# Up projection in seven block products: the fourth product of the gate block summed in PSUM, one pair late, with two PSUM pairs in turn

## What is computed

```python
def conv_ffn(hn, buf, w_up, conv_w, conv_b, w_down):
    T = hn.shape[1]
    up = hn @ w_up
    full = jnp.concatenate([buf.astype(up.dtype), up], axis=1)
    conv = sum(full[:, j:j + T] * conv_w[j] for j in range(CONV_W)) + conv_b
    a, gt = jnp.split(conv, 2, axis=-1)
    return (a * jax.nn.silu(gt)) @ w_down, full[:, T:]
```

## Time and profile before

| | us |
|---|---|
| median of 3 runs | 2200.4 |
| profiled execution, its own time | 2205.06 |
| span in its profile (first to last instruction) | 2203.1 |
| TensorE busy in the span | 2145.4 (97%) |
| VectorE busy | 1267.4 (58%) |
| ScalarE busy | 754.8 (34%) |
| GpSimd busy | 444.6 (20%) |
| mean granted TensorE clock | 0.99 |

### The profile page before, as it was taken

The page is one execution under the profiler, slowest core; times in us unless marked ns, Lnnn a source line. Parts: engine busy times, 40 slices in busy tenths (PEclk is TensorE's granted clock), DMA queues, the critical chain, the costliest instruction groups (busy, mean ns, idle before and its releaser), DMA issues.

```text
span 2203.1 us, 35662 instructions
## 1 busy us (share of the span) xinstructions
PE 2145.4 (97%) x15110; PEld 2090.6 (95%) x15110; DVE 1267.4 (58%) x1576; ACT 754.8 (34%) x1094; POOL 444.6 (20%) x552
## 2 busy tenths in 40 slices
PE   7999999999999999999999999999999999999997
PEld 6999999999999999999999998999999999999997
DVE  6514756335456354236643233489999999864446
ACT  6313334333422322233322034254444444421113
POOL 6689920000000000000000000023232332200001
PEclk9999999999999999999999999999999999999999
DMA  7321215122431223245412143222222222343212
GB/s 274 120 76 65 69 45 186 50 88 78 146 109 67 87 79 108 87 144 180 142 43 77 58 173 154 96 74 72 81 67 81 67 80 82 130 154 125 86 67 77
DMA packets 66419, 222.78 MB, mean 101 GB/s; under 512 B 7584, under 2 KB 13136, under 8 KB 62576
## 3 DMA queue, kind: packets, MB, share of 16 engines
q1 hardware_dynamic: 46432, 130.15, 17.6%
q0 software_dynamic: 14688, 62.06, 7.5%
q10 hardware_dynamic: 5184, 28.98, 3.5%
HBM read 168.38 MB, written 51.78 MB: 100 GB/s over the span
## 4 chain that ended last, share of the span: by engine, by line
PE 71%; DVE 21%; issue 3%; ACT 2%; POOL 2%; DMA 1%; DVEq 0%; POOLq 0%; ACTq 0%
PE ps L305 19%; PE ps L308 19%; PE ps L306 19%; DVE WQ L3170 4%; DVE CA L3218 3%; DVE CA L3217 3%; POOL WX L2711 2%; PE ps L1981 1%; PE ps L2337 1%; PE ps L2313 1%; DVE UBG L2717 1%; DVE HOUT L3227 1%; DVE CA L3220 1%; DVE UBG L3210 1%; DMA WRAW<-in_wslabs 1%
## 5 line engine op out<-in xcount | busy, mean ns | idle before, releaser
L305 PE MATMUL ps<-XH,WH 128*128 128x352 f32 (+1 forms) x1752 | 567.1, 325 | 5.6 <-ACT STAGE L365 3.1
L306 PE MATMUL ps<-XL,WH 128*128 128x352 f32 (+1 forms) x1560 | 492.5, 321 | 0.0
L308 PE MATMUL ps<-XH,WL 128*128 128x352 f32 (+1 forms) x1752 | 371.5, 320 | 0.0
L305 PEld LDWEIGHTS ps<-XH,WH 128*128 128x128 f32 x1752 | 330.5, 189 | 14.3 <-issue 10.2
L299 DVE TENSOR_TENSOR WL<-WRAW,WH 128x1024 fp32r<-128x1024 f32 x133 | 166.7, 1253 | 271.7 <-ACT WH L294 270.2
L306 PEld LDWEIGHTS ps<-XL,WH 128*128 128x128 f32 x1560 | 294.8, 189 | 0.1
L308 PEld LDWEIGHTS ps<-XH,WL 128*128 128x128 f32 x1752 | 292.9, 189 | 0.0
L294 ACT ACTIVATE WH<-WRAW 128x1024 fp32r<-128x1024 f32 x133 | 140.8, 1058 | 330.0 <-PE ps L308 311.9
L305 PE MATMUL ps<-HX,WH 128*128 128x352 f32 (+1 forms) x480 | 153.6, 321 | 4.7 <-DVE HX L3231 3.7
L306 PE MATMUL ps<-HX,WH 128*128 128x352 f32 (+1 forms) x480 | 151.5, 321 | 0.0
L2777 PE MATMUL ps<-B,WQ 128*128 128x258 f32 x528 | 141.0, 288 | 2.9 <-DVE UBG L3210 2.4
(11 more groups left out here) (619 smaller groups left out, 4752.3 us busy)
## 6 DMA issues: line engine op xcount, KB each, us to landing
WRAW<-in_wslabs SPq DMA_DIRECT2D x133, 512.0 KB, 3.6
WRAW<-in_wup SPq DMA_DIRECT2D x88, 256.0 KB, 2.7
scratch_spill<-STAGE SPq DMA_DIRECT2D x40, 516.0 KB, 2.7
ZS<-scratch_spill POOLq DMA_DIRECT2D x24, 516.0 KB, 5.3
scratch_h<-HOUT ACTq DMA_DIRECT2D x22, 516.0 KB, 2.9
HRAW<-scratch_h POOLq DMA_DIRECT2D x22, 516.0 KB, 5.8
XIN<-in_xT SPq DMA_DIRECT2D x8, 516.0 KB, 4.6
XR<-in_xT ACTq DMA_DIRECT2D x2, 2064.0 KB, 8.6
```

What stands on the lines that cost most here:

```text
L305: pe.matmul(out[t], WH[:, slot, w, :], xh(k, t), start=(k == 0), stop=False)
L306: pe.matmul(out[t], WH[:, slot, w, :], xl(k, t), start=False, stop=False)
L308: last = pe.matmul(out[t], WL[:, slot, w, :], xh(k, t), start=False, stop=(k == nk - 1))
```

## The change

`P4` no longer has banks of its own. It is added in PSUM to `P1+P6+P7` of its pair, so that one instruction reads the finished quarter. The sums of successive pairs use banks 4, 5 and banks 6, 7 in turn. TensorE's order becomes `P1(f) P5(f) P4(f-1) P6(f) P3(f) P7(f) P2(f)`: `P4` of a pair comes after the first two products of the next one. The take of `P7` and join c go. The gate is scaled in two pieces: its second half behind join a3 (`scale_gate`), its first half by the instruction that reads PSUM (`finish_gate`). The work is put in a new order on ScalarE, VectorE and GpSimd, and `P5`, `P4`, `P1` wait for other things.

```diff
-        PAIR = {"P1": 4, "P6": 4, "P7": 4, "P5": 2, "P3": 2, "P2": 0, "P4": 6}
+        def bank_of(p, f):
+
+            return {"P5": 2, "P3": 2, "P2": 0}.get(p, 4 + 2 * (f % 2))
```

SyncE's loads and GpSimd's sums (the sum on `A21` in place goes behind the second `WX`; the first load of a pair waits for all four sums):

```diff
                 sp.wait_ge(s_lo, W_AT["P1", f - 1])
-                sp.wait_ge(s_sum.sem, s_sum.at(4 * f - 1))
+                sp.wait_ge(s_sum.sem, s_sum.at(4 * f))
                 quarter(f, 0)
...
             nc.gpsimd.tensor_tensor(WY, WX, A11, ALU.subtract).then_inc(s_sum.sem, 1)
-
-        def pool_late_sums(pool, f):
-
-            nc.gpsimd.tensor_tensor(A21, A21, A11, ALU.subtract).then_inc(s_sum.sem, 1)
             pool.wait_ge(u_raw[3].sem, u_raw[3].at(16 * (f + 1)))
             pool.wait_ge(s_lo, W_AT["P5", f])
             pool.wait_ge(s_sum.sem, s_sum.at(4 * f + 2))
             nc.gpsimd.tensor_tensor(WX, A12, WY, ALU.subtract).then_inc(s_sum.sem, 1)
+            nc.gpsimd.tensor_tensor(A21, A21, A11, ALU.subtract).then_inc(s_sum.sem, 1)
```

TensorE:

```diff
-                    start, stop = k == 0 and p in ("P1", "P5", "P2", "P4"), k == 3
+                    start, stop = k == 0 and p in ("P1", "P5", "P2"), k == 3
...
+            pe.wait_ge(s_lo, W_AT["P1", 1])
+            product("P1", 1)
             pe.wait_ge(s_lo, W_AT["P4", 0])
+            pe.wait_ge(u_dv, DV_AT["a3", 0])
+            product("P4", 0, lambda k: pe.wait_ge(e_lo, E_AT["N4", k]))
+            pe.wait_ge(s_lo, W_AT["P5", 1])
+            pe.wait_ge(u_dv, DV_AT["d2", 0])
+            product("P5", 1)
...
+            rest_of_quad(0, 1)
+            with pe.Fori(0, (NF - 2) // 2) as i:
+                for f in range(2, 4):
+                    pe.wait_ge(s_lo, i * 14 + W_AT["P1", f])
+                    pe.wait_ge(u_rb.sem, u_rb.at(i * 4 + (2 * f - 2)))
+                    product("P1", f)
+                    pe.wait_ge(s_lo, i * 14 + W_AT["P5", f])
+                    pe.wait_ge(u_dv, i * 6 + DV_AT["d2", f - 1])
+                    product("P5", f)
+                    pe.wait_ge(s_lo, i * 14 + W_AT["P4", f - 1])
+                    pe.wait_ge(u_dv, i * 6 + DV_AT["a3", f - 1])
+                    product("P4", f - 1)
+                    rest_of_quad(i, f)
```

ScalarE, the loop:

```diff
             for f in range(1, NF):
-                act_product_hi(act, "P4", f)
+                more = f < NF - 1
+                if f > 1:
+                    act_product_hi(act, "P7", f)
+                    act_product_hi(act, "P2", f)
+                    act.wait_ge(u_cv.sem, u_cv.at(2 * f - 3))
+                else:
+                    act_take(act, "P1", 1, first_half(UB[1][0]))
+                    act_product_hi(act, "P6", 1)
+                    act_product_hi(act, "P3", 1)
                 now(f - 1, 0)
                 if f > 1:
+                    act_take(act, "P1", f, first_half(UB[f % 2][0]))
+                    if more:
+                        act_product_hi(act, "P1", f + 1)
                     act.wait_ge(u_cv.sem, u_cv.at(2 * f - 2))
-                act_take(act, "P1", f, first_half(UB[f % 2][0]))
...
+                act_take(act, "P5", f, second_half(UB[f % 2][1]))
...
+                act_product_hi(act, "P4", f)
                 now(f - 1, 1)
-                act_take(act, "P5", f, second_half(UB[f % 2][1]))
-                if f < NF - 1:
+                act_take(act, "P6", f, second_half(UB[f % 2][0]))
+                if more:
                     act_product_hi(act, "P5", f + 1)
...
                 silu(f - 1)
-                if f < NF - 1:
+                if more:
+                    act_product_hi(act, "P6", f + 1)
                     act_product_hi(act, "P3", f + 1)
```

VectorE, the two new pieces and the loop:

```diff
+            def scale_gate(f):
+                u = UB[f % 2][1][:, 2 + HALF:2 + N]
+                dve.wait_ge(u_dv, DV_AT["a3", f])
+                L(nc.vector.tensor_tensor(u, u, RB[:, HALF:N], M))
+
+            def finish_gate(f):
+                dve.wait_ge(u_pe, U_AT["P4", f])
+                nc.vector.tensor_tensor(first_half(UB[f % 2][1]), pair("P4", f), by_bank(RB[:, 0:HALF]), M).then_inc(u_rb.sem, 1)
...
             for f in range(1, NF):
+                more = f < NF - 1
+                dve_product_lo(dve, "P7", f)
+                dve_product_lo(dve, "P2", f)
+                if more:
+                    dve_product_lo(dve, "P1", f + 1)
+                convolve(f - 1, 0)
+                finish_gate(f - 1)
                 dve_product_lo(dve, "P4", f)
-                convolve(f - 1, 0)
-                if f < NF - 1:
-                    dve_product_lo(dve, "P1", f + 1)
                 convolve(f - 1, 1)
-                if f < NF - 1:
+                if more:
                     dve_product_lo(dve, "P5", f + 1)
-                    dve_product_lo(dve, "P6", f + 1)
-                join("d2", f)
-                if f < NF - 1:
-                    dve_product_lo(dve, "P3", f + 1)
                 else:
                     slab_lo(0)
-                join("a3", f)
-                if f < NF - 1:
-                    dve_product_lo(dve, "P7", f + 1)
-                join("b", f)
-                dve_scale(dve, f, 0)
...
+                join("d2", f)
+                product(f - 1)
+                if more:
+                    dve_product_lo(dve, "P6", f + 1)
...
+                join("a3", f)
+                scale_gate(f)
+                if more:
+                    dve_product_lo(dve, "P3", f + 1)
...
+                join("b", f)
+                scale_first(f)
```

More of the change, by code:

```diff
@@ L2731, in pool_ffn @@
                     pool_sums(pool, 0)
-                    pool_late_sums(pool, 0)
             pool_sums(pool, 1)
-            pool_late_sums(pool, 1)
             pool.dma_start(O["buf1"], I["buf1"]).then_inc(gl_out, 16)
-            for f in range(1, NF):
-                if f < NF - 1:
[L2738 to L2747, removed]
+            for f in range(2, NF):
+                pool_sums(pool, f)
+            pool.wait_ge(h_out.sem, h_out.at(16 * 4))
+            pool.wait_ge(u_pe, U_AT["P6", NF - 1])
+            for kk in range(2):
+                pool_load_h(pool, 0, kk)
+            pool.wait_ge(u_pe, U_AT["P3", NF - 1])
+            for kk in range(2, 4):
+                pool_load_h(pool, 0, kk)
             pool.wait_ge(h_out.sem, h_out.at(16 * 8))
@@ L2767, in pe_ffn, with product @@
         def pe_ffn(pe):
-            def product(p, w, k_wait=None):
-                x = OPS[OP_OF[p]]
+            def product(p, f, k_wait=None):
+                x, w, bank = OPS[OP_OF[p]], slot_of(p, f), bank_of(p, f)
                 for k in range(4):
@@ L2802, in pe_ffn @@
             evacuated(pe, G_CO + 7)
-            product("P1", slot_of("P1", 0))
+            product("P1", 0)
             pe.wait_ge(s_lo, W_AT["P5", 0])
@@ new lines, in pe_ffn, with rest_of_quad @@
+            pe.wait_ge(u_dv, DV_AT["a3", 0])
[3 more added lines that the diff above has]
+            product("P5", 1)
+            def rest_of_quad(i, f):
+                pe.wait_ge(s_lo, i * 14 + W_AT["P6", f])
+                pe.wait_ge(u_ac, i * 6 + (3 * f + 1))
+                product("P6", f)
+                pe.wait_ge(s_lo, i * 14 + W_AT["P3", f])
+                pe.wait_ge(u_ac, i * 6 + (3 * f + 2))
+                product("P3", f)
+                pe.wait_ge(s_lo, i * 14 + W_AT["P7", f])
+                pe.wait_ge(u_ac, i * 6 + (3 * f + 3))
+                product("P7", f)
+                pe.wait_ge(s_lo, i * 14 + W_AT["P2", f])
+                pe.wait_ge(u_dv, i * 6 + DV_AT["b", f - 1])
@@ L2856, in pe_ffn @@
+            pe.wait_ge(s_lo, W_AT["P4", NF - 1])
+            pe.wait_ge(u_dv, DV_AT["a3", NF - 1])
+            product("P4", NF - 1)
+            pe.wait_ge(u_rb.sem, u_rb.at(2 * NF - 2))
             pe.wait_ge(u_dv, DV_AT["b", NF - 1])
@@ L2965, in act_take @@
             act.wait_ge(u_pe, U_AT[p, f])
-            nc.scalar.activation(to, pair(p), ACT.Copy).then_inc(u_ac, 1)
+            nc.scalar.activation(to, pair(p, f), ACT.Copy).then_inc(u_ac, 1)
         def act_before_up(act):
@@ L3309, in dve_ffn @@
                     slab_lo(1)
-                join("c", f)
-                dve_scale(dve, f, 1)
+                join("b", f)
+                scale_first(f)
             for kk in range(2, 4):
@@ L3314, in dve_ffn @@
             convolve(NF - 1, 0)
+            finish_gate(NF - 1)
             convolve(NF - 1, 1)
```

121 lines of the change are left out of this document (41 added, 80 removed).

## The result

The changed kernel takes **2225.6 us** (median of 4 runs, 2223.84 to 2227.7), the kernel before, on the same chip, 2200.1 us (2196.86 to 2200.54). The ratio is 1.0118, interval 1.0106 to 1.013: 25.5 us slower. The forecast was 2224.

A forecast was written before the change was run, and what follows sets the result against it. VectorE's round was taken to bound the loop: -0.43 - 1.25 + 2.0 + 0.81 = +1.13 us each. With the ends, 5.0 + 19 x 1.13 - 2.9 = +23.6 us, giving 2224 us, range 2197 to 2241.

The forecast's parts named there:

- The bound: In the loop over 22 pairs, VectorE's own round sets the pace, 21.08 us a loop; TensorE's floor is 20.36 us.
- Step 1, the work: In each loop on VectorE, join c and the whole gate's scale go, `scale_gate` and `finish_gate` come: net -0.43 us.
- Step 2, the waits: In each loop, VectorE's 1.25 us wait before P3's low part goes; two waits for ScalarE come, +1.2 and +0.8 us.
- Step 3, the turns: In each loop, GpSimd's four sums hold up VectorE 3.66 us against 2.85 before, +0.81 us; bounds 0 and 5.2.
- Step 4, the ends: Outside the loops: start up to pair 1's value scale +5.0 us, pair 20's scale to first XD add -2.9 us.
- VectorE under TensorE's floor: Rival: in the loop, sums land in VectorE's new waits and beside joins, TensorE paces at 20.36 us, 2189 us; chance 0.14.
- The clock: Rival: the new waits in the loop lower TensorE's clock, 23.4 us a loop, 2247 us; chance 0.06.

The follow-up runs named there:

- e4: The changed kernel with GpSimd's four sums cut to 8 of each 512 columns from the third pair on: 2188.3 us, ratio 0.9945.
- e5: The kernel before the change, with GpSimd's four sums cut to 8 of each 512 columns from the third pair on: 2180.9 us, ratio 0.9906.
- e6: e3 with GpSimd's sum on A21 put back behind the sum WY: 2187.6 us, ratio 0.9932.
- e1: The changed kernel with ScalarE taking P1 and making the next high part of P1 ahead of the value's `now`: 2201.1 us, ratio 1.0006.
- e2: The changed kernel with VectorE running `finish_gate` ahead of the value's convolution instead of behind it: 2215.2 us, ratio 1.0077.
- e8: e6 with P4(0) back ahead of P1(1), pair 0's joins d2, a3 earlier, and two ScalarE high parts ahead of its take: 2184.2 us, ratio 0.9934.
- e3: The changed kernel with the edits of both e1 and e2: 2190.8 us, ratio 0.9957.
- e7: The changed kernel with only GpSimd's sum on A21 put back behind the sum WY: 2221.1 us, ratio 1.0089.

## Why the prediction was right

By its own steps:

- **The bound** held. VectorE's round sets the loop in both kernels; TensorE's waits follow from it. Cutting GpSimd's sums short, which changes neither TensorE's nor ScalarE's order, brings either kernel to TensorE's floor (e4, e5). The floor was put at 20.36 us; it is 20.2 (e4, e5, e6). PEld was busy 386.59 us in the stretch of the earlier trace rows and 383.73 us in that of e5 with as many weight loads within two, so a load takes 0.8% longer where waits are between; what makes it longer isn't shown.
- **Step 1, the work**, -0.43: `finish_gate` takes 0.60 (1627.81 to 1628.41) as put, join a3 to the scale 0.71 and the scale 0.73 (1639.78, 1640.49, 1641.22), put at 0.72 each.
- **Step 2, the waits**, +1.2 and +0.8: 1.17 and 0.72 in the timeline; taken away they are worth 1.26 (e1) and 0.52 (e2). The old wait of 1.25 us behind L2711 is gone, as put.
- **Step 3, the turns**, 3.66 against 3.73 us. Three of the four hits are where they were put: 0.94 forecast and 0.90 measured, 0.6 and 0.74, 1.08 and 1.09. The sum WY hit a copy of 10 columns for 1.00 us, and not L3217 for 1.04, which by the new order has already run: there the size came out by luck. The Trainium skill ("SBUF — State Buffer", Who interferes with whom) says that the port pair is locked for the whole instruction; by that rule the turns would have come to up to 5.2 us. The trace agrees with the rule: what is held up goes on when the other engine's instruction ends (1633.58 and 1633.56, 1635.05 and 1635.01 above), and in e2 an 8-column step that starts with the sum takes 1.32 us where the sum takes 1.29. The turns stay below 5.2 us because VectorE's instructions arrive when part of the sum is over; the prediction had named only joins and idle time as the reason, and took the rows to show less than the rule.
- Summed: -0.43 - 1.25 + 1.89 + (3.73 - 2.85) = +1.09, and measured +1.13. The 2.85 for the kernel before is a little low: it takes L3219's mean of 0.26 us for an 8-column step alone, where one that meets nothing has 0.23; with 0.23 for both lines it is 2.96, and the sum +0.98.
- **Step 4, the ends**: +5.45 for +5.0 and -2.6 for -2.9. Its cause was named too narrowly, as e8 shows: the size was right, the slot that P6(1) shares with P4(0) is only part of it. The start held two waits of TensorE that the forecast gave no size, 2.85 us ahead of P1(1) and 3.35 ahead of P7(1); without the second, in e2, the start was no shorter. The rows are three waits of PEld, and then the stretches behind the last two (columns as the earlier trace rows); half the clock was granted behind the second:

```profile
1477.76 0.19 PEld L2768 LDWEIGHTS ps<-B,WQ 128*128 128x128 f32 x1 [2.85 <-DVE WQ L3176]
...
1497.12 0.29 PEld L2768 LDWEIGHTS ps<-N,WQ 128*128 128x128 f32 x1 [3.35 <-issue]
...
1966.63 0.19 PEld L305 LDWEIGHTS ps<-HX,WH 128*128 128x128 f32 x1 [4.01 <-issue]
```

```profile
1497.00:1502.00 5.00, 4.84 (x22) 4.88 (x23) 4.86 (x6) 1.66 (x3) 2.96 (x2) 0.50 0.18 48
1966.63:1972.63 6.00, 5.97 (x28) 6.00 (x29) 3.37 (x4) 1.15 (x2) 0.00 (x0) 0.72 0.49 168
```

- **Missed**: the 1.6 us behind the first XD add. TensorE, freed of its wait for HX, stands 4.01 us there instead of 1.25 and starts again at 0.72 of the clock instead of 1.00 (last lines above). In those 6 us TensorE loads weights 29 times, in the 6 us behind the 1.25 us of the kernel before 39 times; ten loads at 6.5 to the us are 1.5 us. It is small, and the argument had looked for clock losses in the loop only.
- **The rivals.** VectorE under TensorE's floor did not come by itself, since the sums fell on busy VectorE and not on its waits; its price was about right: e3, which gets there, takes 2190.8 against the 2189 put. The clock: TensorE's waits of some 0.85 us (ahead of P6) and 1.04 us (ahead of P7) in each loop left it at 1.00, and e3, without them, gained what VectorE's two waits measure. The Trainium skill ("TensorE: Matmul & The Clock Gate", A second HAM failure mode: psum-queue depth-cycling) tells of a kernel whose matmul groups have small idle times between them so often that the clock keeps going down and up; the section that the prediction names, the one before it, has longer waits, for loads. Nothing of the kind showed in this loop.

## What to carry to other kernels

Before you take work off an engine that looks like the bound, ask which engine's round closes the loop, and write that round out step by step with its waits. Here a join less, with the scale cut in two, was worth 0.43 us a loop, while two hand-overs that stood one place too late cost 1.8; with a take and a high part earlier on ScalarE and one instruction earlier on VectorE, 25 us of loss became 9 us of gain (13 with the old order of the sums). An instruction that another engine waits for belongs ahead of the next instruction that waits for that engine.

## What the runs showed of the hardware that was not expected

- What a GpSimd sum of 128x512 (1.29 us) costs the VectorE instruction that meets it goes by how much of the sum is left, not by the instruction's own size. It was 1.00 us on a copy of 10 columns (0.17 alone) with 1.13 us of the sum left, 0.90 on an 8-column step (0.23 alone) with 1.11 left, 1.09 on such a step with all of it left (e2), 1.09 on a 512-column low part with 1.23 left, and 0.48 and 0.74 on the product of 1032 columns with 0.62 (e7) and 0.88 left. Instructions that read PSUM and one SBUF tensor stay at 0.68 to 0.69 us beside the same sums. Cut to 8 columns (0.21 to 0.51 us on average in e4, 0.21 to 0.92 in e5), the four sums cost VectorE nothing that shows in its timeline.
- The clock behind a single wait isn't set by the wait's length alone. TensorE stood 2.52 us before the same weight load in e3 and in e7; over the 6 us from the end of the wait on it was granted 0.72 in the one and 1.00 in the other:

```profile
1929.95:1935.95 6.00, 5.97 (x29) 6.00 (x30) 3.37 (x4) 1.15 (x2) 0.00 (x0) 0.72 0.45 150
```

```profile
1958.19:1964.19 6.00, 5.97 (x38) 6.00 (x39) 3.40 (x5) 1.15 (x2) 0.00 (x0) 1.00 0.48 163
```

That is worth 1.5 us: behind the first XD add e3 takes 260.6 us, e7 259.1. The wait before this one, 18 us earlier, was 3.44 us in e3 and 2.35 in e7; whether that is the reason isn't shown.
